# The even layer's gated norm, its output product and the odd norm, regrouped by chunks of columns and by norm group

## The reference

```python
def gated_group_rmsnorm(y, z, w):
    g = (y * silu(z)).reshape(bsz, L, SSD_GROUPS, W // SSD_GROUPS)   # 2 groups of 512
    g = g * rsqrt(mean(g * g, axis=-1, keepdims=True) + EPS)
    return g.reshape(bsz, L, W) * w
...
    y_b = gated_group_rmsnorm(y, ssd_z, ssd_norm)
    mixed = concatenate([y_a, y_b], axis=-1)
    return h + mixed @ w_out
...
    u = rmsnorm(h, norm_w)                  # odd layer
    q, k, v, g = split(u @ w_in, 4, axis=-1)
```

## Time and profile before

| | us |
|---|---|
| median of 3 runs | 4285.78 (4281.91 to 4288.18) |
| the profiled execution's own time | 4290.72 |
| its span | 4288.9 |
| PE busy | 4016.5, 94% of the span |
| DVE, ACT, POOL busy | 1869.1, 1372.6, 1474.5 |
| mean granted TensorE clock | 0.971 of 2.4 GHz |

### The profile page before, as it was taken

How to read it: one execution, slowest core, us unless ns; L and a number is a source line. 1 busy time by engine, 2 the same in 40 slices (tenths; PEclk the granted TensorE clock), 3 DMA queues, 4 the chain that set the end, 5 groups by cost and what they waited for, 6 DMA issues and landing times.

```text
span 4288.9 us, 49187 instructions
## 1 busy us (share of the span) xinstructions
PE 4016.5 (94%) x20614; PEld 3226.5 (75%) x20614; DVE 1869.1 (44%) x2707; ACT 1372.6 (32%) x2142; POOL 1474.5 (34%) x895
## 2 busy tenths in 40 slices
PE   7999999899999899999999889999868879999998
PEld 5888888665655567888888789999647778888878
DVE  3322323633354444233233656443672206666664
ACT  3111111433322332111112443311221316666663
POOL 2232222234443542223222134322642213343464
PEclk9999999999999999999999999999988999999999
DMA  2111111200000121111111011121102120000013
GB/s 90 50 50 50 50 40 50 75 25 20 25 16 19 45 80 43 45 50 51 48 50 40 25 40 40 60 85 65 33 25 75 45 93 27 27 26 27 27 62 131
DMA packets 57949, 206.06 MB, mean 48 GB/s; under 512 B 7424, under 2 KB 11040, under 8 KB 57344
## 3 DMA queue, kind: packets, MB, share of 16 engines
q1 hardware_dynamic: 45744, 158.55, 11.3%
q0 software_dynamic: 9424, 41.75, 2.6%
q10 hardware_dynamic: 2560, 2.61, 0.2%
HBM read 177.40 MB, written 25.49 MB: 47 GB/s over the span
## 4 chain that ended last, share of the span: by engine, by line
PE 77%; DVE 11%; ACT 5%; POOL 3%; issue 3%; DMA 1%; DVEq 0%; ACTq 0%; POOLq 0%
PE ps L434 15%; PE ps L435 14%; PE ps L436 14%; PE ps L3388 3%; PE ps L3321 2%; POOL wlo L408 2%; PE ps L1582 2%; PE ps L3323 2%; PE ps L3322 2%; PE ps L1583 2%; PE ps L1584 2%; PE ps L778 2%; PE ps L3372 2%; PE ps L3418 2%; PE ps L1682 1%
## 5 line engine op out<-in xcount | busy, mean ns | idle before, releaser
L408 POOL TENSOR_TENSOR wlo<-raw,whi 128x1024 fp32r<-128x1024 f32 x286 | 689.3, 2421 | 804.5 <-ACT whi L399 804.5
L434 PE MATMUL ps<-fxh,whi 128*128 128x512 f32 x1488 | 605.7, 407 | 42.7 <-POOL wlo L408 20.5
L435 PE MATMUL ps<-fxh,wlo 128*128 128x512 f32 x1488 | 582.4, 391 | 0.0
L436 PE MATMUL ps<-fxl,whi 128*128 128x512 f32 x1488 | 581.7, 391 | 0.0
L434 PE MATMUL ps<-xh,whi 128*128 128x352 f32 (+1 forms) x1400 | 471.9, 337 | 45.9 <-POOL xl L630 16.5
L435 PE MATMUL ps<-xh,wlo 128*128 128x352 f32 (+1 forms) x1400 | 454.5, 325 | 0.0
L436 PE MATMUL ps<-xl,whi 128*128 128x352 f32 (+1 forms) x1400 | 453.4, 324 | 0.0
L399 ACT ACTIVATE whi<-raw 128x1024 fp32r<-128x1024 f32 x286 | 294.4, 1048 | 469.4 <-PE ps L436 425.7
L434 PEld LDWEIGHTS ps<-fxh,whi 128*128 128x128 f32 x1488 | 281.2, 189 | 122.3 <-issue 35.7
L1042 POOL TENSOR_TENSOR hl<-t,hh 128x512 fp32r<-128x512 f32 x88 | 113.9, 1295 | 734.1 <-ACT hh L982 734.1
L435 PEld LDWEIGHTS ps<-fxh,wlo 128*128 128x128 f32 x1488 | 281.3, 189 | 68.1 <-issue 12.2
(11 more groups left out here) (387 smaller groups left out, 7706.2 us busy)
## 6 DMA issues: line engine op xcount, KB each, us to landing
raw<-in_w_dram SPq DMA_DIRECT2D x286, 512.0 KB, 3.3
res<-rs_scratch POOLq DMA_DIRECT2D x16, 520.0 KB, 6.0
rs_scratch<-res POOLq DMA_DIRECT2D x2, 4160.0 KB, 13.5
szin<-zs_scratch SPq DMA_DIRECT2D x8, 520.0 KB, 3.2
gs_scratch<-oot POOLq DMA_DIRECT2D x8, 520.0 KB, 5.7
...
oot<-rs_scratch POOLq DMA_DIRECT2D x2, 1408.0 KB, 8.4
...
```

Of the source, the lines that this page charges most:

```text
L408: pool.x.tensor_tensor(K.wlo[n % 3][:, :], K.raw[n % 2][:, :], K.whi[n % 3][:, :], ALU.subtract).then_inc(*S.up("w_lo", n))
L434: pe.x.matmul(out, wh, xh, start=k == 0, stop=False)
L435: pe.x.matmul(out, wl, xh, start=False, stop=False)
L436: last = pe.x.matmul(out, wh, xl, start=False, stop=k == K - 1)
```

## The change

The norm's factor 1/rms is one number for each token and group, so it can be applied after the product. The gated y is multiplied by `ssd_norm_2` alone and split (ACT high part with scale, DVE low part), and goes into the product at once. Each product EB is made in two halves of four k, one for each group, in two banks; DVE multiplies each half by its group's 1/rms, adds the two, and later adds the sum to `res`. Gating goes chunk by chunk on DVE alone. PE makes the sums of squares between the k-steps of the first product of a chunk. The products go in the order of `EB_ORDER`: for each chunk f = 0 to 2 (three units are held), then f = 3 and 4 over all chunks, then for each chunk f = 5 to 7. The odd norm's sums are placed by `EB_SUMS` and `Q_SUMS` behind named products, and the first three gate units go chunk by chunk. POOL restores `res` by chunk. Units EB.0 to EB.2 are split before the scan. The gate tiles have eight places in SBUF instead of two. All earlier stages keep their instructions; the parts of the helpers that nothing called any more are taken out.

```diff
--- before.py
+++ after.py
@@ act_ssd_in, pool_ssd_in: last line of each
+    act_units(act, UNIT_AT["EB.2"])
...
+    pool_units(pool, UNIT_AT["EB.2"])
@@ gated_chains, gated, odd_chains, add_places, pe_add, follow_add, dve_add_rows (and the class Chain with its four generators) are removed
+def _eb_order():
+    head = [(f, c) for c in range(3) for f in range(3)]
+    middle = [(f, c) for f in (3, 4) for c in range(3)]
+    return head + middle + [(f, c) for c in range(3) for f in (5, 6, 7)]
+EB_ORDER = _eb_order()
+EB_SUMS = {(5, 0): [(0, k) for k in range(5)], (7, 0): [(1, k) for k in range(5)], (6, 1): [(0, k) for k in (5, 6, 7)],
+           (5, 2): [(2, k) for k in range(5)], (6, 2): [(1, k) for k in (5, 6, 7)]}
+Q_SUMS = {(1, 0): [(2, k) for k in (5, 6, 7)]}
+def pe_even_out(pe):
+    S, K = pe.S, pe.K
+    scan_end(pe)
+    def gated_sum(c, k):
+        grp = k // 4
+        pe.wait_ge("gated_sq", (c, k))
+        if k % 4 == 0:
+            pe.bank(6 + grp)
+        pe.x.matmul(K.bank(6 + grp, columns(c)[2]), K.m("ones"), gated_square(K, c, k), start=k % 4 == 0,
+                    stop=k % 4 == 3, skip_group_check=True).then_inc(*S.up("pe_gated", (c, k)))
+        pe.banks[6 + grp] = [("gated_root", (c, grp, "v"))]
+    def paced(c):
+        def wait(k):
+            pe.wait_ge("gated_lo", (c, k))
+            if k:
+                gated_sum(c, k - 1)
+        return wait
+    for f, c in EB_ORDER:
+        c0, c1, w = columns(c)
+        i, wh, wl = pe_unit(pe, f"EB.{f}")
+        part = eight(K, wh, wl, c0, c1)
+        wait = paced(c) if f == 0 else None
+        for grp in range(2):
+            b = eb_bank(f, c, grp)
+            pe.bank(b)
+            pe_product(pe, K.bank(b, w), 4, lambda k: part(4 * grp + k), ("EB", f, c, grp),
+                       wait and (lambda k: wait(4 * grp + k)))
+            pe.banks[b] = [("dve_eb", ("mul", f, c, grp))]
+        if f == 0:
+            gated_sum(c, 7)
+        if c == 2:
+            S.freed[i] = "pe_group", ("EB", f, 2, 1)
+        for item in EB_SUMS.get((f, c), ()):
+            pe_odd_sum(pe, *item)
...
+def act_even_out(act):
+    S, K = act.S, act.K
+    scan_end(act)
+    exp_ln(act)
+    def operand(c, k):
+        c0, c1, w = columns(c)
+        y = K.res[:, k, c0:c1]
+        act.wait_ge("gated_y", (c, k))
+        act.x.activation(K.xh[:, k, c0:c1], y, ACT.Copy, scale=K.v("ssd_norm_2", k)).then_inc(*S.up("gated_hi", (c, k)))
+        if 8 * c + k >= 4:
+            act.wait_ge("pe_gated", ((8 * c + k - 4) // 8, (k - 4) % 8))
+        act.x.activation(gated_square(K, c, k), y, ACT.Square).then_inc(*S.up("gated_sq", (c, k)))
+    def root(c, grp):
+        act_root_of(act, "gated", (c, grp), *gated_tiles(K, c, grp))
+    for c in range(3):
+        for k in range(8):
+            operand(c, k)
+            if c and k in (0, 2):
+                root(c - 1, k // 2)
+    root(2, 0)
+    act_units(act, UNIT_AT["EB.3"])
+    root(2, 1)
+    act_units(act, UNIT_AT["EB.7"])
+    for item in EB_SUMS[5, 0] + EB_SUMS[7, 0] + EB_SUMS[6, 1]:
+        act_odd_square(act, *item)
+    act_root_of(act, "odd", (0,), *odd_tiles(K, 0))
+    for k in range(8):
+        act_odd_high(act, 0, k)
+    for item in EB_SUMS[5, 2] + EB_SUMS[6, 2]:
+        act_odd_square(act, *item)
+    act_units(act, UNIT_AT["Q.24"])
+    act_root_of(act, "odd", (1,), *odd_tiles(K, 1))
+    for k in range(8):
+        act_odd_high(act, 1, k)
+        if k == 3:
+            act_units(act, UNIT_AT["Q.25"])
+    act_units(act, UNIT_AT["Q.26"])
+    for item in Q_SUMS[1, 0]:
+        act_odd_square(act, *item)
+    act_root_of(act, "odd", (2,), *odd_tiles(K, 2))
+def act_odd_square(act, c, k):
+    S, K = act.S, act.K
+    c0, c1, w = columns(c)
+    n = ODD_SUM_AT[c, k]
+    act.wait_ge("dve_eb", ("add", k, c))
+    if n >= 4:
+        act.wait_ge("pe_odd_sum", ODD_SUMS[n - 4])
+    else:
+        act.wait_ge("pe_gated", (2, 7))
+    act.x.activation(odd_square(K, c, k), K.res[:, k, c0:c1], ACT.Square).then_inc(*S.up("odd_sq", (c, k)))
+def act_odd_high(act, c, k):
+    S, K = act.S, act.K
+    c0, c1, w = columns(c)
+    act.wait_ge("pe_group", ("EB", 7, c, 1))
+    act.wait_ge("odd_y", (c, k))
+    act.x.activation(K.xh[:, k, c0:c1], K.et[4 + k % 4][:, 0:w], ACT.Copy).then_inc(*S.up("odd_hi", (c, k)))
+def dve_even_out(dve):
+    S, K = dve.S, dve.K
+    scan_end(dve)
+    def gate(c, k):
+        c0, c1, w = columns(c)
+        y = K.res[:, k, c0:c1]
+        dve.wait_ge(f"ld_zin{k}", 0)
+        dve.x.tensor_tensor(y, y, K.szin[k][:, c0:c1], ALU.mult).then_inc(*S.up("gated_y", (c, k)))
+    def low(c, k):
+        c0, c1, w = columns(c)
+        dve.wait_ge("gated_hi", (c, k))
+        dve.x.scalar_tensor_tensor(K.xl[:, k, c0:c1], K.res[:, k, c0:c1], K.v("ssd_norm_2", k), K.xh[:, k, c0:c1],
+                                   ALU.mult, ALU.subtract).then_inc(*S.up("gated_lo", (c, k)))
+    def variance(c, grp):
+        dve.wait_ge("pe_gated", (c, 4 * grp + 3))
+        if c:
+            dve.wait_ge("gated_root", (c - 1, grp, "r"))
+        dve.x.tensor_scalar(gated_tiles(K, c, grp)[1], K.bank(6 + grp, columns(c)[2]), 1.0 / 512, EPS, ALU.mult,
+                            ALU.add).then_inc(*S.up("gated_root", (c, grp, "v")))
+    def root(c, grp):
+        dve_root_of(dve, "gated", (c, grp), *gated_tiles(K, c, grp))
+    def mul(f, c):
+        n, w = EB_AT[f, c], columns(c)[2]
+        T = eb_tile(K, f, c), K.es[n % 2][:, 0:w]
+        if n >= 9:
+            dve.wait_ge("dve_eb", ("add", *EB_ORDER[n - 4 if n >= 13 else n % 4]))
+        if n >= 2:
+            dve.wait_ge("dve_eb", ("sum", *EB_ORDER[n - 2]))
+        for grp in range(2):
+            dve.wait_ge("gated_root", (c, grp, "r"))
+            dve.wait_ge("pe_group", ("EB", f, c, grp))
+            dve.x.tensor_tensor(T[grp], K.bank(eb_bank(f, c, grp), w), gated_tiles(K, c, grp)[0],
+                                ALU.mult).then_inc(*S.up("dve_eb", ("mul", f, c, grp)))
+        dve.wait_ge("dve_eb", ("mul", f, c, 1))
+        dve.x.tensor_tensor(T[0], T[0], T[1], ALU.add).then_inc(*S.up("dve_eb", ("sum", f, c)))
+    def add(f, c):
+        c0, c1, w = columns(c)
+        r = K.res[:, f, c0:c1]
+        dve.wait_ge(f"back_e{c}", 0)
+        dve.wait_ge("dve_eb", ("sum", f, c))
+        dve.x.tensor_tensor(r, r, eb_tile(K, f, c), ALU.add).then_inc(*S.up("dve_eb", ("add", f, c)))
+    def odd_variance(c):
+        dve.wait_ge("pe_odd_sum", (c, 7))
+        if c == 2:
+            dve.wait_ge("odd_root", (0, "r"))
+        elif c < 2:
+            dve.wait_ge("gated_root", (2, c, "r"))
+        dve.x.tensor_scalar(odd_tiles(K, c)[1], K.bank(6 + c % 2, columns(c)[2]), 1.0 / D, EPS, ALU.mult,
+                            ALU.add).then_inc(*S.up("odd_root", (c, "v")))
+    def apply(c, k):
+        c0, c1, w = columns(c)
+        dve.wait_ge("odd_root", (c, "r"))
+        if c or k >= 4:
+            dve.wait_ge("odd_lo", (c, k - 4) if k >= 4 else (c - 1, k + 4))
+        dve.x.scalar_tensor_tensor(K.et[4 + k % 4][:, 0:w], K.res[:, k, c0:c1], K.v("odd_norm_2", k), odd_tiles(K, c)[0],
+                                   ALU.mult, ALU.mult).then_inc(*S.up("odd_y", (c, k)))
+    def odd_low(c, k):
+        c0, c1, w = columns(c)
+        dve.wait_ge("odd_hi", (c, k))
+        dve.x.tensor_tensor(K.xl[:, k, c0:c1], K.et[4 + k % 4][:, 0:w], K.xh[:, k, c0:c1],
+                            ALU.subtract).then_inc(*S.up("odd_lo", (c, k)))
+    def both(f, c):
+        mul(f, c)
+        add(f, c)
+    def odd_norm(c, between):
+        dve_root_of(dve, "odd", (c,), *odd_tiles(K, c))
+        for k in range(8):
+            apply(c, k)
+            if k:
+                odd_low(c, k - 1)
+            if k in between:
+                between[k]()
+        odd_low(c, 7)
+    for c in range(3):
+        for k in range(8):
+            gate(c, k)
+            if k:
+                low(c, k - 1)
+            if k == 6:
+                variance(c, 0)
+            if c:
+                if k == 1:
+                    variance(c - 1, 1)
+                elif k in (2, 4):
+                    root(c - 1, k // 2 - 1)
+                elif k >= 5:
+                    mul(k - 5, c - 1)
+        low(c, 7)
+    root(2, 0)
+    variance(2, 1)
+    root(2, 1)
+    for f in range(3):
+        mul(f, 2)
+    for c in range(3):
+        for f in range(3):
+            add(f, c)
+    for f, c in EB_ORDER[9:19]:
+        both(f, c)
+    odd_variance(0)
+    both(6, 1)
+    odd_norm(0, {3: lambda: both(7, 1), 7: lambda: both(5, 2)})
+    both(6, 2)
+    both(7, 2)
+    odd_variance(1)
+    odd_norm(1, {})
+    odd_variance(2)
+    odd_norm(2, {})
+def pool_even_out(pool, A):
+    S, K = pool.S, pool.K
+    for c, (c0, c1) in enumerate(CHUNKS):
+        pool.wait_ge("gated_lo", (c, 7))
+        pool.wait_ge("gated_sq", (c, 7))
+        pool.x.dma_start(K.res[:, :, c0:c1], A["rs"][:, :, c0:c1]).then_inc(*S.up(f"back_e{c}", 0, 16))
```

(68 more changed lines are left out.)

418 lines of the change are left out of this document (89 added, 329 removed).

## The result

The changed kernel takes **4237.9 us** (median of 4, 4237.4 to 4242.7) beside 4287.0 of the kernel before (median of 4, 4281.9 to 4293.8): ratio 0.9887, 95% interval 0.9876 to 0.9899. Forecast were 4232.0 us in a range of 4216 to 4254. The profiled execution has a span of 4235.6 us and a granted clock of 0.976.

The account below looks back on a forecast made before the run. TensorE, busy 94% of 4288.9 us, bounds the kernel. From 4290.7, less 54.3 (fewer waits after the scan), plus 0.5 (scan entry), gives 4236.9; less 4.9 for execution above median, 4232 us, range 4216 to 4254.

Parts of the forecast that it names:

- Start and price of the work: From the scan's end: TensorE starts at half clock, a loss of 2.5 us; its work stays 211.3 us.
- three independent things that hide: In the rest of EB: restore DMAs, weight units and DVE's adds run hidden behind TensorE's products.
- Short gaps of chunks 1 and 2: Even norm: TensorE waits for a bank (0.3), k=6 (1.4) and k=7 (0.9), 5.2 us for both chunks.
- rival B: TensorE's clock falls again in short gaps of chunks 1 and 2: about +8 us, 4240; chance 0.12.
- First and second new wait: Odd norm: TensorE idles 6.4 us for ACT's squares, 8.8 for Q.25's low part; with half clock 9.2 and 11.3.
- Rival A: The two waits on ACT's order do not bite: 20.5 us less, 4211.5; chance 0.12.
- Sum of the stretch: TensorE's start to last gate product: 211.3 us of work plus 28.2 us of waits, 54.3 us gained.
- Scan entry: EB.2's low part on POOL ahead of the scan slows DVE's small ops: 0.5 us, bounds 0 and 2.4.
- C: After the scan, DVE's two-input ops become the bound at 0.86 us each: +19 us, 4251; chance 0.03.
- D: Nothing gained: the freed time reappears at the spill behind the last gate store; chance 0.03.

Follow-up runs that it names:

- full-width gating: The changed kernel with the gating multiply over all 1040 columns in the loop of chunk 0 and none in chunks 1 and 2: 4233.9 us.
- the repeat: The changed kernel itself, run again without an edit as a control: 4239.3 us.

## Why the prediction was right, point by point

**Start and price of the work.** 2.6 us from the first gating multiply to TensorE, forecast 2.5. The clock's rise behind the start I had put at 5.1 us; the rows that I took it from give 5.7 (3189.49 to 3195.19), and here the first 0.32 us record stands 4.4 us behind TensorE's start, at 3175.67. Work at full clock and three independent things that hide (restores, EB's units, adds) came as said; the dense window 3230 to 3286 is busy for 56.0 of 56.0 us. The forms cost what they had cost before: gating 0.50 to 0.52 us busy, multiply from PSUM 0.52.

**Short gaps of chunks 1 and 2.** Forecast 5.2 us, measured 4.2 (4.0 and 0.2), at the places named, k=6 and k=7 (1.41 and 0.58, 1.43 and 0.61; forecast 1.4 and 0.9). What I left out is the half clock behind them. That is rival B in small: the clock did fall, briefly, in each of chunks 1 and 2, and full-width gating showed the price, 3.1 us (11.2 to 8.1 in the table) and not the rival's 8. (What the repeat's 12.3 has more lies at the start and behind the two long waits, not in these chunks.) The Trainium skill's warning (TensorE: Matmul & The Clock Gate, "HAM oscillation") is told there of bursts with DMA waits between them, longer ones than these gaps; here it is borne out in kind by gaps of at most 1.43 us, against my reading of the rows.

**First and second new wait.** 6.4 and 8.2 us against 6.4 and 8.8, for the reasons given. The first went when TensorE's sums were put two products later, the second when copies and squares were put ahead on ACT, and the stretch fell by 8.2 and 10.0 against 9.2 and 11.3 counted with their half clock. Rival A (they do not bite) is out.

**Sum of the stretch.** 211.3 + 28.2 + 2.5 us were to take it from the scan's end to 242.0; it took 243.9. Gaps were 1.6 less (18.8 against 20.4), half clock 3.4 more (11.2 against 7.8), nearly all of that the clock in chunks 1 and 2.

**Scan entry.** The step that was wrong, by its size: I took 0.5 us within 0 to 2.4, it cost 1.94. I had averaged over how much of GpSimd's operation the small DVE operations would overlap. Here they did not share: the one that starts 0.25 us behind it ends 0.17 us after it is over. By the Trainium skill's rule (SBUF — State Buffer, "SBUF: two separate sides") the loser waits for the whole instruction; here the trace agrees. By that rule the entry was to cost up to 2.4 us, and this was nearer than my 0.5.

**From 4232 to 4238.** Stretch +1.9, entry +1.4, spill and the rest +0.9 (823.1 against 822.2 us), and +1.2 from the 4.9 us that I took off because the profiled execution stood so far above its median: the changed kernel's profile reached the end of the scan 1.8 us earlier, with 1.94 added on the way, so that 3.7 of the 4.9 came back. With the 0.5 us between the changed kernel's profile and its median that is the 5.9. Of these only the stretch and the entry (3.3 us) are the change's; the rest is of the size of the wander ahead of the scan. So a median within 6 us of the forecast is in part luck, and 4237.9 is even nearer to rival B's 4240; what speaks for the working is that the gaps stand where they were said, within 1 us of their sizes.

**Rivals C and D.** Gating and low parts took 0.51 and 0.57 us on the mean in the first window, none over 0.59, so C did not come. Its mechanism is there all the same from 3223 on, where GpSimd makes the low parts of the next units (2.40 to 2.77 us):

```profile
3223.63 2.40 POOL L359 TENSOR_TENSOR wlo<-raw,whi 128x1024 fp32r<-128x1024 f32 x1 [2.44 <-ACT whi L350]
3225.09 1.31 DVE L2921 TENSOR_TENSOR gv<-gr,gv 128x336 f32<-128x336 f32 x1 [1.07 <-ACT gr L2914]
```

Behind this root step, sums of 1.76 and 2.54 us, an add of 2.59 and a low part of the odd norm of 2.55 follow, in place of some 0.5 each. TensorE waited for none of them here, since it had products in store or waited longer for something else. For D: the rest behind the last gate, 823.1 us, lies within the scatter of the runs, with 822.2 before.
